# A transformer block on one core: keys scaled without a square root, one low-rank product moved, and the gate's narrow products in two row groups

## The chip, the cores and the metric

The kernel runs on one core of a Trainium2 chip. The metric is the device time of the whole launch in microseconds. A core has five engines that run side by side: TensorE (PE, with its weight loads shown as PEld), VectorE (DVE), ScalarE (ACT), GpSimd (POOL) and SyncE (SP), which mostly issues transfers. They meet only at semaphores. Products land in PSUM, which VectorE and ScalarE empty.

## The reference, cut to what matters

The block projects 512 tokens of 1024 features to many columns (float32 throughout), mixes them by a pooling branch and a recurrent branch of 16 heads of 64 features (RWKV-7), then a gate, an output product and a feed-forward part. The change lies in the recurrent branch:

```python
kk = heads(k * k_k)
kk = kk / jnp.maximum(jnp.linalg.norm(kk, axis=-1, keepdims=True), 1e-12)
k = k * (1 + (a - 1) * k_a)
o = wkv7_scan(rh, heads(decay), kh, vh, kk, heads(a))   # uses -kk and kk * a
...
w = -softplus(-(w0 + tanh(xw) @ w_decay_up)) - 0.5      # low-rank product, K = 64
a = sigmoid(a0 + xa @ w_aaa_up)                         # low-rank product, K = 64
g = sigmoid(xg) @ w_gate_up                             # low-rank product, K = 160 = 128 + 32
...
state = state * w_t + (state @ a_t) b_t + v_t k_t       # a_t = -kk, b_t = kk * a
```

## The kernel before

The recurrence is written in chunks of 64 tokens. Heads are taken four at a time, a *quad* (two pairs of 128 features, q = 0 and 1), and `QUADS` is 4. A pass `it` runs from -1 to 4 and each has 27 slots (`SLOTS`). In one pass each engine does three things: `work`, the chunk algebra of quad `it`; `prep`, the preparation of quad `it + 1` (decays, keys, scaled operands in `At`, `Bt`, `Kt`, `Rt`); and `tail`, the normalisation, the gate and the output rows of quad `it - 1`. Pass -1 has only `prep`, pass 4 only `tail`. Every engine has a function `slot(it, s)` that says what it does there, so the order on each engine is fixed by the code. Between them TensorE does the big input projection in pieces of 12 matmuls (`gemm_piece`, L1824, 128x512 in the reduced float32 form, each weight split in a high and a low part): `PER_SLOT` says how many pieces a slot has (0 to 3). ScalarE makes the high part of a weight tile (L767), GpSimd the low part (L672), and SyncE loads the raw tile.

The small products go to three PSUM buffers, `set0` to `set2`, in turn: the place of a product in `PE_ORDER` modulo 3 is its buffer, and `wait_set_free` makes TensorE wait until whoever reads the product three places earlier is done. So the list sets the order as well as who waits for whom. The names that matter here:

- `lora0`, `lora1` (L1925, L1926): the low-rank products for pair 0 and 1 of the next quad, two matmuls with 64 rows each; `lora_tanh` on ScalarE reads them (L829 into `sg`, L830 into `aa` or `aa_odd`).
- `norm0`, `norm1` (L1933): the squared norm of each head's key by a product with `ones_pair`. Then `norm_root` on ScalarE takes the square root (L837), `norm_inverse` on VectorE clips it and takes the reciprocal (L1276, L1279), and `inv0`, `inv1` on TensorE (L1943) spread the reciprocal over the 64 features. `unit_keys` (L1288) multiplies the key by it into `t1`.
- `bonus` (L1961), read by VectorE at L1399; `D`, `K`, `HD0`, `HD1`, `V1`, `K2`, `TT`, `AP0`, `AP1`: products of the chunk algebra. `K` is read by ScalarE and by VectorE (L1240, the copy with one added, called KI).
- `yT` (L1878, the turned output of the previous quad, in set 2, which `K` had before it) and `gate` (L1979 with 128 rows and L1980 with the other 32, for each q).
- `O` and `TB`, `TK` (L1866) begin a pass. `TB` and `TK` need what GpSimd makes at L704 and L705 from the prepared operands.

## Time and profile before

| | us |
|---|---|
| median of 3 runs | 1071.58 |
| the 3 runs | 1066.44, 1071.58, 1076.22 |
| the profiled execution's own time | 1063.63 |
| its span, first to last instruction | 1061.7 |
| TensorE busy in the span | 969.6 (91%) |
| VectorE, ScalarE, GpSimd busy | 687.6, 467.3, 366.6 |
| mean granted TensorE clock | 0.981 of full speed |

In the profiled execution the passes stand at: preparing pass 72 to 118 us, quad 0 118 to 209, quad 1 209 to 301, quad 2 301 to 397, quad 3 397 to 486, the tail pass to 512. What follows (gates, output product, feed-forward) takes the rest. "Busy" says only that an instruction is under way, and a matmul's end is modelled, so the waits and the start times carry more than the shares. All times below are from the span's start.

### The profile page before, as it was taken

What the parts mean: (1) busy time and instruction counts of PE and PEld (TensorE: products, weight loads), DVE (VectorE), ACT (ScalarE), POOL (GpSimd) and SP (SyncE); (2) the same over time, 40 slices, a digit from 0 to 9 for tenths busy, and PEclk for the clock granted to TensorE, in tenths of its full rate; (3) what the DMA queues carried; (4) which work ended last, traced back from release to release, by engine and by line L of the source; (5) the groups of instructions that cost most, each with busy time, mean ns of one, the idle gap of its engine ahead of it and who ended that gap; (6) DMA issues with size and microseconds to landing.
All of it is one profiled execution on the core that took longest, in us unless ns stands there. A gap on an engine that the chain in (4) does not pass through costs nothing.

```text
span 1061.7 us, 27421 instructions
## 1 busy us (share of the span) xinstructions
PE 969.6 (91%) x11539; PEld 804.7 (76%) x11539; DVE 687.6 (65%) x937; ACT 467.3 (44%) x571; POOL 366.6 (35%) x218
## 2 busy tenths in 40 slices
PE   1798989999999999899999999799999999999994
PEld 1676777777777678667688888688889898898883
DVE  5735667668847866764232255558778787787877
ACT  0335454346435623435532242374644545445351
POOL 7332510411241131124553444235144052350532
PEclk9998998999999999999999999899999999999997
DMA  9332324224332333332344328214152250432201
GB/s 370 105 99 57 89 83 144 63 81 124 92 82 82 112 86 81 114 108 61 120 135 112 128 71 253 56 48 126 35 158 76 82 158 20 138 97 61 80 1 80
DMA packets 122918, 108.03 MB, mean 102 GB/s; under 512 B 5395, under 2 KB 104641, under 8 KB 122817
## 3 DMA queue, kind: packets, MB, share of 16 engines
q1 hardware_dynamic: 113009, 83.46, 26.2%
q10 hardware_dynamic: 9808, 23.08, 7.1%
q8 instruction: 81, 1.33, 0.5%
q14 instruction: 20, 0.16, 0.0%
HBM read 100.23 MB, written 2.10 MB: 96 GB/s over the span
## 4 chain that ended last, share of the span: by engine, by line
PE 46%; issue 21%; DVE 13%; POOL 12%; ACT 3%; DMA 2%; SPq 1%; ACTq 0%; POOLq 0%; DVEq 0%
PE bank L1824 12%; POOL w_lo L737 10%; PE set L2125 6%; PE bank L2125 5%; PE set L1878 4%; PE set L2224 3%; PE set L1866 3%; PE set L1890 2%; PE bank L1805 2%; PE set L1902 1%; PE bank L2261 1%; DMA ada<-in_w_ada_dram 1%; PE bank L2224 1%; DVE Q L1240 1%; DVE acc L1176 1%
## 5 line engine op out<-in xcount | busy, mean ns | idle before, releaser
L672 POOL TENSOR_TENSOR w_lo<-w_raw,w_hi 128x1024 fp32r<-128x1024 f32 (+2 forms) x75 | 171.7, 2290 | 385.1 <-ACT w_hi L767 376.6
L767 ACT ACTIVATE w_hi<-w_raw 128x1024 fp32r<-128x1024 f32 (+2 forms) x81 | 81.8, 1010 | 104.7 <-PE set L2125 35.2
L2186 PE MATMUL set<-a_hi,w_hi 128*128 128x256 f32 x384 | 109.6, 285 | 8.1 <-DVE res L1581 5.4
L796 ACT ACTIVATE Q<-set 128x1024 f32<-128x1024 f32 x56 | 57.5, 1026 | 134.7 <-PE set L1878 69.3
L1824 PE MATMUL bank<-h_hi,w_hi 128*128 128x512 f32 x256 | 108.1, 422 | 3.5 <-POOL w_lo L672 2.6
L2186 PE MATMUL set<-a_lo,w_hi 128*128 128x256 f32 x384 | 108.6, 283 | 0.0
L2186 PE MATMUL set<-a_hi,w_lo 128*128 128x256 f32 x384 | 108.6, 283 | 0.0
L1121 ACT ACTIVATE w_hi<-w_raw 128x1024 fp32r<-128x1024 f32 x70 | 74.3, 1062 | 77.6 <-PE set L2186 63.5
L1824 PE MATMUL bank<-h_hi,w_lo 128*128 128x512 f32 x256 | 102.9, 402 | 1.0 <-issue 1.0
L1824 PE MATMUL bank<-h_lo,w_hi 128*128 128x512 f32 x256 | 103.6, 405 | 0.0
L1581 DVE SCALAR_TENSOR_TENSOR res<-set,mod,res 128x256 f32<-128x256 f32 x192 | 92.9, 484 | 14.9 <-PE set L2186 2.9
L737 POOL TENSOR_TENSOR w_lo<-w_raw,w_hi 128x1024 fp32r<-128x1024 f32 x35 | 89.5, 2557 | 9.2 <-ACT w_hi L1121 5.9
L737 POOL TENSOR_TENSOR w_lo<-w_t,w_hi 128x1024 fp32r<-128x1024 f32 x7 | 16.9, 2417 | 187.1 <-ACT w_hi L1121 187.1
L2186 PEld LDWEIGHTS set<-a_hi,w_hi 128*128 128x128 f32 x384 | 73.6, 192 | 10.1 <-issue 6.6
L2186 PEld LDWEIGHTS set<-a_lo,w_hi 128*128 128x128 f32 x384 | 73.7, 192 | 0.3
L2186 PEld LDWEIGHTS set<-a_hi,w_lo 128*128 128x128 f32 x384 | 73.6, 192 | 0.0
L1824 PEld LDWEIGHTS bank<-h_hi,w_hi 128*128 128x128 f32 x256 | 48.9, 191 | 20.1 <-issue 6.3
L1824 PEld LDWEIGHTS bank<-h_hi,w_lo 128*128 128x128 f32 x256 | 48.9, 191 | 11.3 <-issue 0.7
L1824 PEld LDWEIGHTS bank<-h_lo,w_hi 128*128 128x128 f32 x256 | 49.2, 192 | 9.6 <-issue 0.7
L1533 DVE TENSOR_TENSOR w_lo<-w_raw,w_hi 128x1024 fp32r<-128x1024 f32 x38 | 46.6, 1225 | 11.1 <-ACT w_hi L1121 7.5
L2272 PE MATMUL set<-h_hi,w_hi 128*128 128x512 f32 x128 | 49.8, 389 | 0.0
L2272 PE MATMUL set<-h_lo,w_hi 128*128 128x512 f32 x128 | 49.8, 389 | 0.0
(360 smaller groups left out, 2283.1 us busy)
## 6 DMA issues: line engine op xcount, KB each, us to landing
w_raw<-in_w_ff_dram SPq DMA_DIRECT2D x64, 512.0 KB, 4.2
w_raw<-in_w_in_dram SPq DMA_DIRECT2D x46, 512.0 KB, 3.7
y<-in_w_ada_dram ACTq DMA_DIRECT2D x20, 512.0 KB, 3.8
ada<-in_w_ada_dram SPq DMA_DIRECT2D x16, 512.0 KB, 9.2
Q<-in_w_ada_dram ACTq DMA_DIRECT2D x12, 512.0 KB, 4.1
w_raw<-in_w_rwkv_up_dram SPq DMA_DIRECT2D x8, 512.0 KB, 3.7
w_raw<-in_w_out_dram SPq DMA_DIRECT2D x8, 512.0 KB, 4.5
xtok<-in_x_dram SPq DMA_DIRECT2D x4, 512.0 KB, 9.5
```

What stands on the lines that cost most here:

```text
L672: link(pool.tensor_tensor(part_of(k, w_lo), raw_part(k), part_of(k, w_hi).bitcast(F32), ALU.subtract), "lo_ready")
L737: again(pool.tensor_tensor(w_lo[SLOT[m]][:, :, :], raw[:, :, :], w_hi[SLOT[m]][:, :, :].bitcast(F32), ALU.subtract), "lo_ready")
L767: link(act.activation(part_of(k, w_hi), raw_part(k), ACT.Copy), "hi_ready")
L796: link(act.activation(by_half(tile), psum_flat(set_of(name)), ACT.Copy), "act_kept")
L1121: link(act.activation(w_hi[SLOT[m]][:, :, :], raw[:, :, :], ACT.Copy), "hi_ready")
L1533: link(dve.tensor_tensor(w_lo[slot][:, :, :], raw[:, :, :], w_hi[slot][:, :, :].bitcast(F32), ALU.subtract), "lo_by_dve")
L1581: link(dve.scalar_tensor_tensor(out=res[:, f, tokens], in0=product, scalar=mod[:, 40 + f:41 + f], in1=res[:, f, tokens], op0=ALU.mult, op1 ...
L1824: mm = pe.matmul(o, w, hx, start=(m == 0), stop=(m == 3 * KT - 1))
L1878: mm = pe.matmul(ps[N * p:N * p + N, q, c * C:(c + 1) * C], by_pair(left, p, q, c), by_pair(right, p, q, c), start=(m == 0), stop=(m == le ...
L2125: mm = pe.matmul(o, w[slot_of(k)][:, kt, :], hx[:, kt, :], start=(kt == 0 and m == 0), stop=(kt == kts - 1 and m == 2))
L2186: mm = pe.matmul(to, wx[:, i, columns], a[:, form, i, :], start=OPENS[at] and b == 0 and i == 0 and m == 0, stop=i == 1 and m == 2, skip_g ...
L2272: mm = pe.matmul(bank[m][:, :], w[slot][:, kt, :], hx[:, kt, :], start=(kt == 0 and at == 0), stop=(kt == KT - 1 and at == 2))
```

## The change

Five edits, all in the passes:

1. ScalarE no longer takes the square root (`norm_root` is gone, eight calls). VectorE reads the squared norm from PSUM, clips it at 1e-24 and takes the reciprocal, so `inv` now carries one over the square. `t1` holds the raw scaled key over its square; `At` is the raw scaled key times the decay, and its minus sign has moved to `Bt`. The product of the two operands is the same as before.
2. VectorE's `norm_inverse` stands at the head of slot 6 (it was last in slot 6) for q = 0 and at the end of slot 12 (it was first in slot 14) for q = 1.
3. `lora1` on TensorE goes from slot 11 to slot 8, right behind `inv0` and ahead of three pieces and of `bonus`; its tanh on ScalarE goes from slot 12 to slot 8.
4. `inv1` goes from ahead of `V1` and `K2` to behind them, and `unit_keys(n, 1)` (now `keys_over_square`) behind VectorE's keeping of `K2`.
5. The gate's 32-row remainder of q = 1 lies in rows 32 to 63 (`xg1` has 64 rows, filled by one copying transfer on SyncE's queue), and both remainders are issued together after the two 128-row products.

```diff
-"D1", "KR0", "KR1", "A8T", "D2", "W0", "inv0", "bonus", "D", "lora1", "K", "HD0", "HD1", "yT", "norm1", "gate",
-"inv1", "V1", "K2", "TT", "AP0", "AP1", ...
+"D1", "KR0", "KR1", "A8T", "D2", "W0", "inv0", "lora1", "bonus", "D", "K", "HD0", "HD1", "yT", "norm1", "gate",
+"V1", "K2", "inv1", "TT", "AP0", "AP1", ...
...
-                sp.dma_start(lup[0:DG1, q, 2, :], w_gate_up[0, P:DG, cols]).then_inc(sem("gup_in"), 16)
+                sp.dma_start(lup[DG1 * q:DG1 * (q + 1), q, 2, :], w_gate_up[0, P:DG, cols]).then_inc(sem("gup_in"), 16)
...
+                if k == first_chunk(0):
+                    sp.wait_ge(sem("lora_ready"), 2)
+                    sp.dma_start(xg1[DG1:2 * DG1, :], xg1[0:DG1, :]).then_inc(sem("xg1_twice"), 16)
...
-            def norm_root(it, q):
-                m = 2 * (it + 1) + q
-                wait_made(act, f"norm{q}", it)
-                if m:
-                    act.wait_ge(sem("inverse_ready"), m)
-                link(act.activation(norms[:, :], pset[set_of(f"norm{q}")][:, 0, 0:2 * TB], ACT.Sqrt), "norm_taken")
...
-                dve.wait_ge(sem("norm_taken"), 2 * n + q + 1)
-                link(dve.tensor_scalar(norms[:, :], norms[:, :], 1e-12, None, ALU.max))
+                wait_made(dve, f"norm{q}", n - 1)
+                link(dve.tensor_scalar(norms[:, :], pset[set_of(f"norm{q}")][:, 0, 0:2 * TB], 1e-12 ** 2, None, ALU.max), "norm_taken")
...
-                    link(dve.scalar_tensor_tensor(out=a[:, h, :, 1:C], in0=kk[:, h, :, 1:C], scalar=-1.0, in1=w[:, h, :, 0:C - 1],
+                    link(dve.scalar_tensor_tensor(out=a[:, h, :, 1:C], in0=k[:, h, :, 1:C], scalar=col(90 + m), in1=w[:, h, :, 0:C - 1],
...
                 for q in range(2):
-                    o = pset[set_of("gate")][:, q, :]
-                    pe.matmul(o, lup[:, q, 1, :], xg0[:, :], start=True, stop=False)
-                    mm = pe.matmul(o, lup[0:DG1, q, 2, :], xg1[:, :], start=False, stop=True)
+                    pe.matmul(o[:, q, :], lup[:, q, 1, :], xg0[:, :], start=True, stop=False)
+                for q in range(2):
+                    rows = slice(DG1 * q, DG1 * (q + 1))
+                    mm = pe.matmul(o[:, q, :], lup[rows, q, 2, :], xg1[rows, :], start=False, stop=True)
```

On TensorE, pass 1 (quad 1) from `yT` on, before. Rows are `yT`, `norm1`, the four gate products, `inv1`, then `V1` and `K2` together, and the first matmul of the next piece:

```order
L1878 MATMUL set<-Q,O 64x64 x32
L1933 MATMUL set<-ones_pair,G 128x2 x4
L1979 MATMUL set<-xg,lup 128x512
L1980 MATMUL set<-xg,lup 128x512
L1979 MATMUL set<-xg,lup 128x512
L1980 MATMUL set<-xg,lup 128x512
L1943 MATMUL set<-ident,inverse 64x128 x8
L1866 MATMUL set<-Q 64x64 x64
L1824 MATMUL bank<-h_hi,w_hi 128x512
```

The same place now:

```order
L1869 MATMUL set<-Q,O 64x64 x32
L1924 MATMUL set<-ones_pair,G 128x2 x4
L1971 MATMUL set<-xg,lup 128x512 x2
L1974 MATMUL set<-xg,lup 128x512 x2
L1857 MATMUL set<-Q 64x64 x64
L1934 MATMUL set<-ident,inverse 64x128 x8
L1815 MATMUL bank<-h_hi,w_hi 128x512
```

The remainders have come together, and `inv1` has gone behind `V1` and `K2`.

On VectorE, pass 1 from the keeping of `K` on, before. L1240 is KI, L1269 and L1272 the decay sums, L1466 a term of the next modulation, L1276 and L1279 `norm_inverse`, L1424 and L1426 the output rows with the gate, L1288 `unit_keys`, and the last L1240 keeps `K2`:

```order
L1240 TENSOR_TENSOR Q<-set,Q 128x1024
L1269 TENSOR_SCALAR sg<-sg 128x512
L1272 SCALAR_TENSOR_TENSOR t<-scanm,sg 128x512
L1466 SCALAR_TENSOR_TENSOR y<-Q,derived,y 128x1024
L1276 TENSOR_SCALAR norms<-norms 128x8
L1279 RECIPROCAL inverse<-norms 128x8
L1424 TENSOR_TENSOR y<-y,xvb 128x1024
L1426 TENSOR_TENSOR y<-y,set 128x1024
L1466 SCALAR_TENSOR_TENSOR y<-y,derived 128x1024
L1288 SCALAR_TENSOR_TENSOR t<-G,params,set 128x512
L1240 TENSOR_TENSOR Q<-set,Q 128x1024
```

The same place now:

```order
L1231 TENSOR_TENSOR Q<-set,Q 128x1024
L1260 TENSOR_SCALAR sg<-sg 128x512
L1263 SCALAR_TENSOR_TENSOR t<-scanm,sg 128x512
L1268 TENSOR_SCALAR norms<-set 128x8
L1271 RECIPROCAL inverse<-norms 128x8
L1457 SCALAR_TENSOR_TENSOR y<-Q,derived,y 128x1024
L1415 TENSOR_TENSOR y<-y,xvb 128x1024
L1417 TENSOR_TENSOR y<-y,set 128x1024
L1457 SCALAR_TENSOR_TENSOR y<-y,derived 128x1024
L1231 TENSOR_TENSOR Q<-set,Q 128x1024
L1280 SCALAR_TENSOR_TENSOR t<-G,params,set 128x512
```

`norm_inverse` has gone ahead of the modulation term, and the keeping of `K2` ahead of the keys.

## Rows read from the trace of the kernel before

**Rows 1.** Windows: us, then busy us (count) of PE, PEld, DVE, ACT, POOL; clock, DMA, GB/s.
```profile
72.00:118.00 46.00, 41.89 (x199) 32.59 (x198) 26.84 (x38) 22.63 (x28) 16.59 (x7) 0.93 0.26 72
...
209.00:301.00 92.00, 87.92 (x2050) 67.81 (x2042) 66.67 (x81) 46.74 (x53) 22.80 (x10) 1.00 0.34 98
```
**Rows 2.** Waits of TensorE, whole span: for what, us in total, times, longest.
```profile
PE set L1943 <- issue: 4.7, 2, 3.1
PE set L1943 <- DVE inverse L1279: 4.1, 2, 2.1
PE set L1878 <- DVE Q L1240: 4.0, 3, 2.3
...
PE set L1902 <- ACT aa_odd L830: 2.5, 2, 1.3
```
**Rows 3.** Timeline, preparing pass and quad 0: start, us, engine, operation, [idle before and releaser].
```profile
87.97 0.50 PE L1824 MATMUL bank<-h_hi,w_hi 128*128 128x512 f32 x1 [2.00 <-POOL w_lo L672]
...
97.61 0.95 PE L1933 MATMUL set<-ones_pair,G 128*128 128x2 f32 x8
98.62 1.28 ACT L837 ACT_TABLE_LOAD   x1 [2.31 <-PE set L1933]
...
100.20 0.17 DVE L1276 TENSOR_SCALAR norms<-norms 128x8 f32<-128x8 f32 x1 [1.98 <-ACT norms L837]
...
100.66 0.48 PE L1943 MATMUL set<-ident,inverse 128*64 128x128 f32 x2 [2.11 <-DVE inverse L1279]
...
116.41 2.23 POOL L705 TENSOR_TENSOR Q<-Q,DC 128x1024 f32<-128x1024 f32 x1
...
118.47 0.34 PE L1866 MATMUL set<-Q 64*64 64x64 f32 x8
...
177.36 1.09 PE L1943 MATMUL set<-ident,inverse 128*64 128x128 f32 x16 [1.95 <-DVE inverse L1279]
```
**Rows 4.** Windows, columns as in Rows 1, around stretches of half clock and one without.
```profile
100.70:107.00 6.30, 6.30 (x26) 5.01 (x27) 2.99 (x6) 3.72 (x5) 2.36 (x1) 0.50 0.31 86
...
157.00:161.80 4.80, 4.77 (x16) 3.68 (x16) 1.99 (x3) 0.00 (x0) 1.58 (x1) 0.64 0.44 120
...
177.40:181.90 4.50, 4.50 (x145) 4.21 (x145) 2.16 (x2) 3.33 (x5) 1.99 (x1) 0.64 0.24 60
...
304.00:306.00 2.00, 0.20 (x13) 0.20 (x16) 0.00 (x0) 1.94 (x3) 0.00 (x0) 1.00 0.06 12
306.00:310.00 4.00, 4.00 (x95) 3.31 (x92) 1.39 (x2) 0.44 (x1) 2.40 (x1) 1.00 0.01 4
```
**Rows 5.** Timeline of quad 1, from the bonus to `yT`.
```profile
250.95 1.22 DVE L1399 TENSOR_TENSOR xvb<-set,xvb 128x1024 f32<-128x1024 f32 x1 [1.70 <-PE set L1961]
...
259.19 1.10 PE L1902 MATMUL set<-Q 64*64 64x128 f32 x32 [1.27 <-ACT aa_odd L830]
...
262.73 1.23 DVE L1240 TENSOR_TENSOR Q<-set,Q 128x1024 f32<-128x1024 f32 x1
...
264.10 1.16 PE L1878 MATMUL set<-Q,O 64*64 64x64 f32 x64 [0.86 <-DVE Q L1240]
```
**Rows 6.** Timeline of TensorE: bonus (quad 0), low-rank pair (quad 1), gate (quad 1).
```profile
161.84 1.88 PE L1961 MATMUL set<-G,ones_head 128*128 128x512 f32 x4
163.65 1.16 PE L1866 MATMUL set<-Q 64*64 64x64 f32 x64
...
217.84 0.69 PE L1925 MATMUL set<-xwa,lup 64*128 64x512 f32 x1
217.85 0.69 PE L1926 MATMUL set<-xwa,lup 64*128 64x512 f32 x1
...
266.10 1.10 PE L1979 MATMUL set<-xg,lup 128*128 128x512 f32 x2
267.14 1.12 PE L1980 MATMUL set<-xg,lup 32*128 32x512 f32 x2
...
270.30 1.09 PE L1943 MATMUL set<-ident,inverse 128*64 128x128 f32 x16
```

More of the change, by code:

```diff
@@ L84, in build @@
         w_raw += same_place(("w_raw2", [P, KT, P], F32), ("w_raw3", [P, KT, P], F32))
-        xg0, xg1 = sb("xg0", [P, S]), sb("xg1", [DG1, S])
+        xg0, xg1 = sb("xg0", [P, S]), sb("xg1", [2 * DG1, S])
         lup = sb("lup", [P, 2, 3, P])
@@ L225, in build @@
         PE_ORDER = ["TB", "TK", "O", "BR0", "BR1", "lora0", "mod", "AT0", "AT1", "TV", "AD0", "AD1", "A2T", "norm0", "A4", "A4T",
-                    "D1", "KR0", "KR1", "A8T", "D2", "W0", "inv0", "bonus", "D", "lora1", "K", "HD0", "HD1", "yT", "norm1", "gate",
-                    "inv1", "V1", "K2", "TT", "AP0", "AP1", "MR0", "MR1", "N", "OI", "S1", "S2", "S3", "S4", "S5", "S6"]
+                    "D1", "KR0", "KR1", "A8T", "D2", "W0", "inv0", "lora1", "bonus", "D", "K", "HD0", "HD1", "yT", "norm1", "gate",
+                    "V1", "K2", "inv1", "TT", "AP0", "AP1", "MR0", "MR1", "N", "OI", "S1", "S2", "S3", "S4", "S5", "S6"]
         BY_ACT = ["TB", "TK", "LT0", "LT1", "TV", "A2T", "A4T", "D1", "D2", "W0", "D", "K", "HD0", "HD1", "V1", "TT", "AP0", "N", "OI"]
@@ L896, in slot @@
                     keep_pair(b1, b2, "AP0", it)
-                if s == 14 and prep:
-                    norm_root(it, 1)
                 k = landing(it, s)
@@ L953, in slot @@
                         link(act.activation(flat_blocks(At), flat(O), ACT.Square), "o_squared")
+                    if prep:
+                        lora_tanh(it, 1)
                 if s == 10 and prep:
@@ L1303, in scaled_reads @@
                     wait_made(dve, "KR1", n - 1)
-                kk, w = (t.rearrange("p (h c t) -> p h c t", h=2, t=C) for t in (t1[:, :], t4[:, q, :]))
+                k, w = (t.rearrange("p (h c t) -> p h c t", h=2, t=C) for t in (xk[:, q, :], t4[:, q, :]))
                 a = one_g(At, q).rearrange("p h (c t) -> p h c t", t=C)
                 for h in range(2):
-                    link(dve.scalar_tensor_tensor(out=a[:, h, :, 1:C], in0=kk[:, h, :, 1:C], scalar=-1.0, in1=w[:, h, :, 0:C - 1],
+                    link(dve.scalar_tensor_tensor(out=a[:, h, :, 1:C], in0=k[:, h, :, 1:C], scalar=col(90 + m), in1=w[:, h, :, 0:C - 1],
                                                   op0=ALU.mult, op1=ALU.mult))
-                link(dve.tensor_scalar(a[:, :, :, 0:1], kk[:, :, :, 0:1], -1.0, None, ALU.mult))
+                link(dve.tensor_scalar(a[:, :, :, 0:1], k[:, :, :, 0:1], col(90 + m), None, ALU.mult))
             def scaled_writes(n, q):
@@ L1313, in scaled_writes @@
                 link(dve.scalar_tensor_tensor(out=a[:, :], in0=a[:, :], scalar=1.0, in1=t1[:, :], op0=ALU.add, op1=ALU.mult))
-                link(dve.scalar_tensor_tensor(out=one_g(Bt, q), in0=tokens(a[:, :]), scalar=0.5, in1=tokens(t3[:, :]), op0=ALU.mult, op1=ALU.mult))
+                link(dve.scalar_tensor_tensor(out=one_g(Bt, q), in0=tokens(a[:, :]), scalar=-0.5, in1=tokens(t3[:, :]), op0=ALU.mult, op1=ALU.mult))
                 link(dve.tensor_tensor(one_g(Kt, q), tokens(t2[:, :]), tokens(t3[:, :]), ALU.mult), "prepared")
@@ L1379, in slot @@
                 if s == 6:
+                    if prep:
+                        norm_inverse(n, 0)
                     if work:
@@ L1382, in slot @@
                         keep_plus_one(b4, "A4T", "A4I", it)
-                    if prep:
-                        norm_inverse(n, 0)
                 if s == 7:
@@ L1417, in slot @@
                         decay_sums(n, 1)
+                        norm_inverse(n, 1)
                 if s == 14:
-                    if prep:
-                        norm_inverse(n, 1)
                     if tail:
@@ L1427, in slot @@
                 if s == 15:
-                    if prep:
-                        unit_keys(n, 1)
                     if work:
                         keep_plus_one(b5, "K2", "K2", it)
+                    if prep:
+                        keys_over_square(n, 1)
                 if s == 16:
@@ L1973, in out_gate @@
                 pe.wait_ge(sem("lora_ready"), 2)
+                pe.wait_ge(sem("xg1_twice"), 16)
                 if it == QUADS:
@@ L1976, in out_gate @@
                 wait_set_free(pe, "gate", it)
+                o = pset[set_of("gate")]
                 for q in range(2):
-                    o = pset[set_of("gate")][:, q, :]
-                    pe.matmul(o, lup[:, q, 1, :], xg0[:, :], start=True, stop=False)
-                    mm = pe.matmul(o, lup[0:DG1, q, 2, :], xg1[:, :], start=False, stop=True)
+                    pe.matmul(o[:, q, :], lup[:, q, 1, :], xg0[:, :], start=True, stop=False)
+                for q in range(2):
+                    rows = slice(DG1 * q, DG1 * (q + 1))
+                    mm = pe.matmul(o[:, q, :], lup[rows, q, 2, :], xg1[rows, :], start=False, stop=True)
                 signal(mm, "gate", it)
@@ L2043, in slot @@
                         inverse_norm(it, 0)
+                        lora(it, 1)
                 if s == 9 and work:
@@ L2049, in slot @@
                     to_pairs("D", it, [(std(b5), b6)])
-                if s == 11 and prep:
-                    lora(it, 1)
                 if s == 12 and work:
@@ L2079, in slot @@
                         to_pairs("K2", it, [(b2, b1)])
+                    if prep:
+                        inverse_norm(it, 1)
                 if s == 17 and work:
```

11 lines of the change are left out of this document (2 added, 9 removed).

## The prediction

> **What bounds the kernel now.** I read the windows first, one for each pass. TensorE is busy 41.9 of 46 us in the preparing pass and 87.9 of 92 in quad 1, where VectorE has 66.7 and ScalarE 46.7 [rows 1]. So TensorE is the bound, and what the change can win are its own instructions, its waits, and the time in which it runs at half clock. ScalarE is half idle, so its freed time counts only where TensorE waits for it. Next come TensorE's waits by releaser: 4.1 us on `inverse` ahead of `inv1`, 4.0 on VectorE's L1240, nearly all ahead of `yT`, 2.5 on ScalarE's `aa_odd` ahead of `HD1`, and 4.7 in the middle of L1943 that nothing in the trace explains [rows 2]. Then the timeline round each of them, and the clock in windows. At full clock the pieces' matmuls run at their pace; three stretches of clock 0.50 to 0.64 (half speed, 1.2 of 2.4 GHz, for part of the window) stand behind gaps of 2.11, 3.1 and 1.95 us on TensorE, of which two are the waits for `inverse` [rows 2 to 4]. A stall of about 2 us at 304 had no such sequel: the clock stayed at 1.00 [rows 4].
>
> The parts, costed against the profiled execution (1063.63 us). It lies 8 us under the median of the three runs, 1071.58, and I know no row for those 8 us; I subtract the sum from the median.
>
> **Preparing pass.** Four things go. (a) ScalarE takes `norm0`'s root, with its table load, ahead of a weight tile in its order, and TensorE waits 2.00 us for that tile at 87.97 [rows 3]. Without the root ScalarE needn't wait for `norm0` there and saves the load's 1.28 and the root, and `lora1`, about 1.05 us, now fills the place ahead of that tile. Gain 2.0. (b) `norm1` ends at 98.56; the table load (1.28), the root and two VectorE instructions make `inv1` start at 100.66. Now VectorE reads the sums itself: from the end of the product to the end of the second instruction about 0.5 us, from L1276's 0.17 twice and the steps between. Gain 2.11 - 0.5 = 1.6. (c) The stretch of 6.30 us at half clock begins in this gap; at full clock its work takes 3.15. Gain 3.15 if the clock holds, 0 if it falls all the same. I take the gain, since the gap shrinks by three quarters. Together TensorE alone would gain 6.7. (d) But quad 0 also needs GpSimd's L705, which ends at 118.64, a sixth of a microsecond after TensorE starts `TB` and `TK` at 118.47 [rows 3]. That chain starts at `inv1`, through VectorE's keys, so it moves by what `inv1` moves: its start 3.6 earlier (2.0 + 1.6) and its length about 0.9 shorter, as it no longer runs at half clock (1.09 for the same product at 177.36, against about 2); and the second table load, ahead of ScalarE's exponents, goes too (up to 1.28). That is 4.5 to 5.5. **The gain of the pass is the smaller one: 5.0.** The ends are 2 (only one wait goes) and 6.7.
>
> A page of the Trainium skill, "ScalarE: Activation LUTs", section "What ACT_TABLE_LOAD costs", puts each switch of table set at about 2.66 us, the load of 1.28 and a drain of 1.38. Row and page agree on the load; the drain isn't here, for the load starts right behind the product it waits for and the clipping on VectorE 1.58 us after the load [rows 3]. By the page 16 loads would be 43 us of ScalarE in place of 21; the sum would be the same by either, as only the waits of TensorE enter it.
>
> **Quad 0.** The same pattern without a gate between `norm1` and `inv1`: TensorE waits 1.95 us for `inverse` at 177.36, and 4.50 us follow at a mean clock of 0.64 [rows 3, 4]. Now `V1` and `K2` (2 us) stand between the two, and `inverse` is ready about 1.7 us after `norm1`: VectorE must first end the decay sums. The wait goes. At full clock the 4.50 us hold 2.9 of work. **Gain 1.95 + 1.6 = 3.5**, between 2.0 and 3.6.
>
> **Gate, quads 0 to 3.** The four products of one gate take 4.20 us, from 266.10 to 270.30, 1.05 each, whether 128 or 32 rows [rows 6]. Afterwards there are two 128-row products in a row, as in the bonus: 1.81 us from its start to the next product's [rows 6]. Then the two remainders. The trace has no pair of 32-row products. Its nearest rows are the low-rank pair, in two groups of 64 rows, which start 0.01 apart [rows 6] and cost 1.05 in all. So a gate costs 1.81 + 1.05 = 2.86 if the remainders run side by side, a gain of 1.34; one behind the other, 1.81 + 1.81 = 3.62, a gain of 0.6. I take 1.3, as the pair is of the same kind: other rows, another PSUM bank. The page "TensorEngine Tiling (Array Packing)", section "Key Properties", says that a change of tiling mode drains TensorE, and that tiles execute in parallel. This case's rows speak for a small drain: 1.05 for a product that follows another shape against 0.9 in the bonus. By the page's word the gate wins twice, by two switches fewer and by the pairing, which is the 2.86 above.
>
> **Where the gate's gain goes.** In quad 3's pass (its `yT` belongs to quad 2) nothing of the preparation runs, and TensorE goes on with `V1` and the pieces at once: 1.3 won. In the tail pass the next thing TensorE waits for is the pool weights' transfer, issued by SyncE after GpSimd's low part of another tile; that isn't moved, so I count 0 (end: 1.3).
>
> **Quads 1 and 2: `lora1` ahead of `bonus`.** Here a wait takes another's place. `HD1` waited 1.27 us for `aa_odd` in each (set 1, which `lora1` had); now `lora1` is read long before, and that wait goes. But `bonus` comes one low-rank pair later, 1.05 us. VectorE waits for it (1.70 us at 250.95) and from there works without a break for 11.8 us until KI at 262.73, and `yT` needs KI because it takes the set of `K`: TensorE already waits 0.86 there [rows 5]. So `yT` starts 1.05 later against `bonus`'s old time, although TensorE is there 1.05 + 1.27 earlier. The wait ahead of `yT` becomes 0.86 + 1.27 + 1.05 = 3.2 us. Behind `yT` the gate is 1.3 shorter, `V1` and `K2` are free at once, and `inv1` waits for the gate's reader on VectorE (about 1.3 us after the gate's end, under `V1` and `K2`). **Net for each of the two: +1.05 - 1.3 = -0.3, together -0.5.** VectorE's earlier `norm_inverse` in slot 6 puts two instructions (0.4 us) ahead of the copy that KR0's buffer waits for; KR1 waits for ScalarE's copy anyway, so 0.1 at most, and I leave it out.
>
> **The clock behind the new wait.** A wait of 3.2 us is as long as the gap of 3.1 that was followed by half clock, 4.80 us at a mean of 0.64, a cost of 1.7; the gap of 2 us at 304 had none [rows 2, 4]. I count one fall in the two quads: +1.7. Ends: none, and two stretches as long as the one at 100.70, +3.15 each.
>
> **The rest costs nothing.** `xg1`'s copy is one transfer on SyncE's queue ahead of the loads of chunk 11, issued in the preparing pass, while the first gate stands at 266 [rows 6]; it delays one raw tile by one issue, with the tile before it already loaded. VectorE's keys have the same count and shapes, only a column in place of -1.0. ScalarE loses 8 roots and 16 table loads (26 loads become 10), under TensorE's work everywhere but in the two places above.
>
> **Sum.** -5.0 - 3.5 - 1.3 - 0 - 0.5 + 1.7 = **-8.6 us**, which is 1063.0 from the median (1055.0 from the profiled time). Some 1%, 10.7 us, is what a measurement of this kernel tells from no change.
>
> **Rivals.**
> (A) *The clock holds everywhere* (25%). Neither new wait lets it fall, the tail's 1.3 comes through, and the preparing pass gives its 6.7: -6.7 - 3.5 - 2.6 - 0.5 = -13.3, so 1058.3. For it: two of the waits that precede half clock are gone. Against it: the new wait is longer than either.
> (B) *The gaps weren't the bound* (15%). VectorE and GpSimd hold the preparing pass's end, it gives only 2, quad 0 gives its wait alone (2.0), the rest as above: -2 - 2 - 1.3 - 0.5 + 1.7 = -4.1, so 1067.5. The start of `TB` beside L705's end speaks for it.
> (C) *The remainders don't run side by side* (8%): 0.7 less in each of quads 1 to 3, 2.1 in all: -6.5, so 1065.1.
> (D) *VectorE becomes the bound from `bonus` on, and the clock pays for it: slower than before* (9%). The place is the wait ahead of `yT` in quads 1 and 2. It decides if half clock follows in both, and long, 6.3 us each (+6.3), while the preparing pass's stretch stays (its gain falls to 2), quad 0's stays too (2.0 left) and the remainders run apart (+2.1): -4 - 1.3 - 0.5 + 2.1 + 6.3 = +2.6. With the bonus late in quad 0 too (+1.05) it is about +4, so 1075. For a loss of over 1% further unexplained stalls as those in L1943 (4.7 us in two) would have to come on top; that such stalls move with any change of the instruction stream is the mechanism I can't price.
> My forecast has the other 43%.
>
> **How the numbers follow.** The cases lie between 1058 and 1075, and the scatter of the runs (1066.44 to 1076.22) is 5 us to each side; the range that leaves 2 in 10 out is 1052 to 1072. Faster by over 1%: nearly all of A and a part of the forecast, 0.39. Slower by over 1%: a small part of D, 0.07. Within 1%: the rest, 0.54.
>
> **What would show it.** Right: no gap between `norm1` and `inv1` in the preparing pass over 0.7 us, clock 1.00 from 98 to 107, and quad 0 beginning some 5 us earlier; no wait at `inv1` in quad 0; a gate of 2.9 us from its first product to the next; no wait ahead of the second `HD` and about 3 us ahead of `yT` in quads 1 and 2; ScalarE about 22 us less busy. Wrong: a gate of 3.6 us or more; half clock still there behind `norm1`; VectorE reaching KI without waiting for `bonus`; or a difference that comes from stretches after 520 us, which the change doesn't touch.

## The result, and the profile after

The changed kernel took **1078.46 us** (median of 7 runs, 1073.36 to 1079.59) against 1067.63 for the kernel before in the same round (7 runs, 1065.54 to 1076.22). The ratio is 1.008, 95% interval 1.0051 to 1.0109: slower by about 1%, where I had forecast 1063.0 and at most 1072. The profiled execution is the fastest of the seven, 1073.36 us with a span of 1071.4 and a mean clock of 0.974, against 1063.63, 1061.7 and 0.981.

First the windows of the passes, columns as in [rows 1].

```profile
72.00:118.00 46.00, 41.66 (x199) 32.50 (x198) 29.96 (x38) 17.23 (x22) 15.76 (x7) 0.93 0.26 74
118.00:209.00 91.00, 84.82 (x2108) 67.46 (x2106) 59.12 (x71) 37.42 (x43) 27.04 (x12) 1.00 0.34 99
209.00:303.00 94.00, 86.58 (x1867) 66.87 (x1866) 66.90 (x78) 39.67 (x46) 22.41 (x10) 0.96 0.33 93
303.00:407.00 104.00, 95.59 (x2060) 74.89 (x2059) 67.82 (x80) 41.14 (x47) 23.07 (x11) 0.90 0.30 85
```

ScalarE is lighter as planned (17.2 in place of 22.6 us in the first window), VectorE heavier by 3 us there. The clock column holds the news: 0.96 and 0.90 in quads 1 and 2, where it was 1.00. From `TB` to `TB`, the preparing pass ends 0.9 us later than before (119.34 against 118.47), quad 0 takes 3.5 less (86.7 against 90.25), quad 1 takes 5.6 more (98.05 against 92.5), quad 2 takes 9.0 more (104.3 against 95.3), and quad 3 with the tail 2.2 less. The 0.9 us are there before the pass begins: TensorE waits 17.1 us for its first transfer in place of 16.1, and ScalarE's high part of the same weight tile starts at 73.54 in place of 72.64. Counted from there the preparing pass takes the same in both kernels. From TensorE's last gate on the rest of the kernel takes the same (554.8 us in both).

TensorE's waits of the first 525 us (as in [rows 2]):

```profile
PE set L1869 <- DVE Q L1231: 9.3, 3, 3.6
...
PE set L1934 <- issue: 4.9, 3, 2.3
PE set L1934 <- DVE inverse L1271: 3.8, 1, 3.8
...
PE set L1857 <- DVE norms L1268: 2.0, 3, 0.8
```

The wait for `aa_odd` ahead of `HD1` is gone, the one ahead of `yT` has grown from 4.0 to 9.3 us in three, and the one for `inverse` is now a single one of 3.8. The last row is new: a product waits until VectorE has read the sums.

The preparing pass (timeline of TensorE, VectorE and GpSimd, put in order of time; [rows 3] before):

```profile
91.41 2.65 POOL L675 TENSOR_TENSOR w_lo<-w_raw,w_hi 128x1024 fp32r<-128x1024 f32 x1 [7.54 <-ACT w_hi L770]
91.84 3.01 DVE L1299 SCALAR_TENSOR_TENSOR Q<-G,params 128x252 f32<-128x252 f32 x2
94.89 2.46 DVE L1301 TENSOR_SCALAR Q<-G,params 128x8 f32<-128x8 f32 x1
94.92 2.40 POOL L675 TENSOR_TENSOR w_lo<-w_raw,w_hi 128x1024 fp32r<-128x1024 f32 x1 [0.87 <-ACT w_hi L770]
96.96 0.95 PE L1924 MATMUL set<-ones_pair,G 128*128 128x2 f32 x8
...
101.28 0.17 DVE L1268 TENSOR_SCALAR norms<-set 128x8 f32<-128x8 f32 x1
...
101.75 0.48 PE L1934 MATMUL set<-ident,inverse 128*64 128x128 f32 x2 [3.84 <-DVE inverse L1271]
...
119.34 0.87 PE L1857 MATMUL set<-Q 64*64 64x64 f32 x44
```

`norm1` ends at 97.91, yet VectorE reads the sums only at 101.28: it has no wait ahead of that row, it is behind. Its instructions ran beside GpSimd's low parts: an operation on 8 columns took 2.46 us and ended with the low part, the pair on 252 columns took 3.01 and ended 0.8 us behind the other. The same pair takes 1.00 and the same small operation 0.23 in quad 1.

Why the low parts fall there can be read on ScalarE, which makes the high part that each of them needs. The rows of the same weight tile (the tenth high part), before and now:

```profile
100.13 1.06 ACT L767 ACTIVATE w_hi<-w_raw 128x1024 fp32r<-128x1024 f32 x1
```
```profile
93.72 1.06 ACT L770 ACTIVATE w_hi<-w_raw 128x1024 fp32r<-128x1024 f32 x1 [1.70 <-PE bank L1815]
```

Before, the root of `norm1` stood ahead of this high part in ScalarE's order and held it until 100.13, when VectorE's long stretch was over. Without the root it comes 6.4 us earlier, and its low part meets VectorE (94.92). The low part of the tile before comes 1.4 us later than before (91.41 against 89.99). In the kernel before one VectorE instruction was held too: 1.98 us at 91.22 in place of 0.75.

Quad 1, from the bonus to the products behind the gate, and the gate of quad 3's pass at full clock ([rows 5, 6] before):

```profile
250.85 1.22 DVE L1391 TENSOR_TENSOR xvb<-set,xvb 128x1024 f32<-128x1024 f32 x1 [2.74 <-PE set L1952]
255.71 1.93 PE L1893 MATMUL set<-Q 64*64 64x128 f32 x64
262.81 1.22 DVE L1231 TENSOR_TENSOR Q<-set,Q 128x1024 f32<-128x1024 f32 x1
264.18 1.62 PE L1869 MATMUL set<-Q,O 64*64 64x64 f32 x64 [3.56 <-DVE Q L1231]
267.45 3.76 PE L1971 MATMUL set<-xg,lup 128*128 128x512 f32 x4
271.14 1.28 PE L1974 MATMUL set<-xg,lup 32*128 32x512 f32 x4
272.36 2.10 PE L1857 MATMUL set<-Q 64*64 64x64 f32 x128
...
464.88 1.98 PE L1971 MATMUL set<-xg,lup 128*128 128x512 f32 x4
466.79 1.13 PE L1974 MATMUL set<-xg,lup 32*128 32x512 f32 x4
467.85 2.10 PE L1857 MATMUL set<-Q 64*64 64x64 f32 x128
```

The gate takes 2.97 us at full clock (464.88 to 467.85), and 4.91 in quad 1. The stretches of half clock behind the waits, as windows ([rows 4] before):

```profile
101.70:108.00 6.30, 6.25 (x27) 5.05 (x28) 3.94 (x7) 1.58 (x3) 0.00 (x0) 0.53 0.01 3
264.10:271.20 7.10, 7.02 (x78) 4.39 (x78) 5.01 (x6) 5.15 (x6) 2.54 (x1) 0.54 0.19 68
...
367.00:381.00 14.00, 13.44 (x216) 9.19 (x218) 9.75 (x10) 6.73 (x8) 2.96 (x1) 0.51 0.30 90
```

**An account.** For each kernel I split the time from 72 us to the tail's first gate product into TensorE's idle stretches over 0.05 us (added up from its timeline), half of the time that the clock record shows at 0.50, and the rest, which is work at full clock. The wait ahead of that gate product is counted in. The windows' mean clock agrees: 0.98 over the 434.87 us of before gives 17 us at half clock, 0.96 over 444.60 gives 36.

| kernel | time in the part | idle | at half clock | work |
|---|---|---|---|---|
| before | 434.9 | 30.9 | 17.1 | 395.4 |
| changed | 444.6 | 35.6 | 34.1 | 392.0 |
| a_lora_back | 432.6 | 30.6 | 20.5 | 391.7 |
| b_lora_only | 463.0 | 36.0 | 71.7 | 391.2 |
| c_gate_only | 434.7 | 32.1 | 20.5 | 392.3 |
| d_root_only | 455.6 | 41.9 | 41.0 | 393.2 |
| i_filled | 435.7 | 28.1 | 20.5 | 397.3 |
| j_no_low | 438.5 | 32.6 | 27.3 | 392.3 |
| k_back_filled | 429.9 | 27.8 | 10.2 | 396.9 |
| l_back_norm | 429.9 | 30.6 | 10.2 | 394.2 |
| m_back_norm_ki | 449.4 | 37.8 | 41.0 | 391.1 |
| o_elsewhere | 445.8 | 31.5 | 30.7 | 398.9 |
| q_both | 431.4 | 26.3 | 17.1 | 396.6 |

Changed against before: work -3.4, idle +4.7, half clock +17.0, which costs 8.5. Together +9.7, as large as the difference of the spans. The work is shorter and the kernel slower. The last column is good to some 4 us only, for where half clock and an idle stretch overlap the time is counted in both: b_lora_only has the old gates and as much work as the kernel before, and shows 4.2 us less; i_filled has 5.6 us more than the changed kernel, and shows 5.3. Each row is one execution. That of the changed kernel is its fastest, with a clock of 0.974; its other six had 0.959 to 0.971.

### The profile page after: what moved, and what is told of

Same layout as the page of the kernel before. It is cut to its first block, busy times and chain, and to the rows that moved or that the text cites. A ratio compares the mean times of both kernels' runs of the same rounds, so it can differ in the third digit from the quotient of the medians.

```text
span 1071.4 us, 27393 instructions
## 1 busy us (share of the span) xinstructions
PE 973.1 (91%) x11539; PEld 809.7 (76%) x11539; DVE 697.9 (65%) x937; ACT 445.3 (42%) x547; POOL 367.3 (34%) x218
## 4 chain that ended last, share of the span: by engine, by line
PE 46%; issue 21%; DVE 14%; POOL 12%; ACT 3%; DMA 2%; SPq 1%; ACTq 0%; POOLq 0%; DVEq 0%
PE bank L1815 11%; POOL w_lo L740 10%; PE set L2118 6%; PE bank L2118 5%; PE set L1869 4%; PE set L2217 3%; PE set L1881 3%; PE set L1857 2%; PE bank L1796 2%; PE set L1796 1%; DMA ada<-in_w_ada_dram 1%; PE bank L2217 1%; PE set L1893 1%; PE bank L2254 1%; PE set L1934 1%
## 5 line engine op out<-in xcount | busy, mean ns | idle before, releaser
L1815 PEld LDWEIGHTS bank<-h_lo,w_hi 128*128 128x128 f32 x256 | 48.9, 191 | 10.6 <-issue 1.7
L1524 DVE TENSOR_TENSOR w_lo<-w_raw,w_hi 128x1024 fp32r<-128x1024 f32 x38 | 46.6, 1225 | 11.1 <-ACT w_hi L1112 7.5
L2265 PE MATMUL set<-h_hi,w_lo 128*128 128x512 f32 x128 | 49.8, 389 | 0.0
```

What stands on the lines that cost most here:

```text
L1524: link(dve.tensor_tensor(w_lo[slot][:, :, :], raw[:, :, :], w_hi[slot][:, :, :].bitcast(F32), ALU.subtract), "lo_by_dve")
L1815: mm = pe.matmul(o, w, hx, start=(m == 0), stop=(m == 3 * KT - 1))
L2265: mm = pe.matmul(bank[m][:, :], w[slot][:, kt, :], hx[:, kt, :], start=(kt == 0 and at == 0), stop=(kt == KT - 1 and at == 2))
```

## The experiments

Each was timed beside the kernel before, which took 1067.59 us (a, b, e, f), 1069.86 (c, d, i, j), 1069.03 (k, l, m, n) and 1069.86 (o, p, q). The first four expectations weigh three theories, W, N and S: the wait ahead of `yT` with half clock behind it; the norm operations too late on VectorE; and stalls that nothing in the trace explains.

**a_lora_back**: the changed kernel with `lora1` back.

```diff
-"inv0", "lora1", "bonus", "D", "K"
+"inv0", "bonus", "D", "lora1", "K"
-                        lora(it, 1)          # slot 8
+                if s == 11 and prep:
+                    lora(it, 1)
```

> The changed kernel with lora1 and its tanh back in their old places (slots 11 and 12, behind D); all else as changed. Theory W (the wait ahead of yT): lora1 ahead of bonus makes VectorE's chain from the bonus to KI late, TensorE waits 3.6 us for it in quads 1 and 2, and half clock follows. Then the wait shrinks to about 2.2 us or less, split between HD1 and yT, half clock in quads 1 and 2 is mostly gone, and the time falls about 8 to 14 us below the changed kernel, that is 1064 to 1070, at or below before. Theory N (the norm operations): the loss comes from VectorE reading the norms late (3.8 us ahead of inv1 in the preparing pass, 0.8 ahead of K2); then the time stays within 3 us of the changed kernel, 1075 to 1079. Theory S (the unexplained stalls that move with the instruction stream): any value between, with the stalls' sum (about 11 us before, 14 after) explaining it.

1063.68 us (12 runs), ratio to before 0.9947 (0.9922 to 0.9972): 14.8 us faster than the changed kernel. The waits ahead of `yT` are 1.05 us, those for `aa_odd` ahead of `HD1` 1.26 again. The move of `lora1` is what made the change slow; the other four edits gain 4 us.

**b_lora_only**: the kernel before with that move alone.

> The kernel before with lora1 and its tanh moved alone. Theory W: the wait ahead of yT grows from 0.9 to about 3.2 us in quads 1 and 2 with half clock behind it, no gain from the gate: 8 to 14 us slower than before, 1076 to 1082. Theory N: same as before within 3 us, 1066 to 1071. Theory S: no telling, with the sum of the unexplained stalls showing it.

1090.48 us (6 runs), ratio 1.0181 (1.0138 to 1.0223). Its waits and windows behind the two `yT`s:

```profile
PE set L1878 <- DVE Q L1240: 9.3, 3, 3.4
PE set L1943 <- DVE inverse L1279: 7.1, 2, 5.0
```
```profile
269.60:286.70 17.10, 16.93 (x224) 10.50 (x224) 7.81 (x10) 6.36 (x8) 2.75 (x1) 0.50 0.34 101
378.80:392.50 13.70, 13.70 (x116) 7.35 (x120) 6.53 (x8) 5.49 (x8) 2.75 (x1) 0.50 0.26 77
```

That is 8 us above the range of theory W. The two waits are those of the changed kernel (3.38), the half clock behind them lasts far longer, and there are more waits with half clock behind them that W had not foreseen: 5.0 us ahead of `inv1` in quad 0 (6.8 us of it) and 2.56 ahead of quad 3's `yT` (13.7). The idle sum grows by 5.1 us only; the clock costs 27.

**e_ki_early**: the changed kernel, KI ahead of `scaled_writes`.

```diff
-                if s == 11 and prep:
-                    scaled_writes(n, 0)
-                if s == 12:
+                if s == 11:
                     if work:
                         keep_plus_one(b4, "K", "KI", it)
+                    if prep:
+                        scaled_writes(n, 0)
```

> The changed kernel with VectorE's KI (and ScalarE's keeping of K, ahead of one transfer's issue) moved ahead of the three scaled writes and one modulation term, so that KI comes about 3 us earlier while lora1 stays ahead of bonus. Theory W: the wait ahead of yT falls from 3.6 to under 1 us, the half clock behind it goes, and the time falls 8 to 14 us, to 1064 to 1070. Theory N: unchanged within 3 us. Theory S: change only as the stalls' sum changes.

1077.96 us (11 runs), ratio 1.008 (1.0053 to 1.0107): nothing. The wait ahead of `yT` went and came back behind the gate:

```profile
PE set L1935 <- DVE y L1418: 7.8, 2, 3.9
```

L1418 is the gate's reader. From the bonus to it VectorE works through one chain, so what `yT` no longer waits for, `inv1` does. Theory W in its first form, that the place of the wait matters, fell.

**f_pieces**: the changed kernel, three of the weight products' pieces moved from slot 15 to slot 12, so that they run in the wait ahead of `yT`.

```diff
-PER_SLOT = [2, 1, 0, 3, 3, 0, 1, 2, 3, 0, 3, 0, 3, 0, 0, 3,
+PER_SLOT = [2, 1, 0, 3, 3, 0, 1, 2, 3, 0, 3, 0, 6, 0, 0, 0,
```

> The changed kernel with the three pieces of slot 15 moved to slot 12, ahead of yT: TensorE works 2.8 us where it waited. Theory W: the wait ahead of yT falls to about 0.8 us, TensorE's clock holds there, and 5 to 12 us are won, if nothing behind slot 15 waits for VectorE in turn (TT needs K2, which VectorE keeps late; that could give back 2 us a quad). Theory N: unchanged or slower. Theory S: as the stalls fall.

1069.86 us (12 runs), ratio 1.0016 (0.9992 to 1.004): 8.6 faster than the changed kernel. The waits ahead of `yT` are 0.85 and 0.84; new ones of 1.5 to 1.9 us, and one of 3.6 in quad 3's pass, stand behind the gate, where the pieces are missing.

**i_filled**: useless work in the same wait. Nothing that waits is released earlier.

```diff
-both_to_heads("HD1", it, b6, b3, IB)
+both_to_heads("HD1", it, b6, b3, IB, 4 if it in (1, 2) else 1)
```

> The changed kernel, with HD1's 64 products issued four times over in quads 1 and 2 (the same values into the same places), so that TensorE works through about 2.8 of the 3.56 us in which it waited ahead of yT. Nothing that waits is released earlier. Theory W (most of what lora1's move costs is half clock behind that wait): the wait ahead of yT shrinks to 0.8, half clock behind it (6.8 us in quad 1, 20.5 in quad 2 in the profile of the changed kernel) goes for the most part, and the kernel gets 5 to 12 us faster for doing more: 1066 to 1073 against 1078. Theory V (the waits themselves, and VectorE's chain, are the cost): the time stays within 2 us of the changed kernel's, 1076 to 1080, or is longer.

1063.29 us (12 runs), ratio 0.9936 (0.9901 to 0.9971). With 5.6 us more of work (six rounds of 0.93) the changed kernel gets **15.2 us faster**. No wait is left ahead of `yT` (stalls of 1.4 and 1.2 us in the repeated rounds, which nothing in the trace explains, took the rest of it), and the places that ran at half clock run at full:

```profile
264.10:271.20 7.10, 7.10 (x99) 4.94 (x90) 5.49 (x7) 3.72 (x5) 0.00 (x0) 1.00 0.34 106
364.00:378.00 14.00, 14.00 (x309) 10.33 (x308) 12.47 (x15) 7.91 (x9) 4.89 (x2) 1.00 0.49 158
```

The medians differ by 15.2 us. The two profiled executions differ by 7.4 only (1073.36 and 1065.98), the one the fastest of its kernel, the other slower than its median; so the account, which shows 8.9 us between them, doesn't explain the whole of the 15.2.

**p_one_round**: one extra round of `HD1` instead of three.

> The changed kernel with one extra round of HD1's products in quads 1 and 2 in place of three: 0.93 us, so the wait ahead of yT shrinks from 3.56 to about 2.6 us. Theory L (the length of the wait decides how long half clock lasts behind it): a part of the 15 us of three rounds comes back, 4 to 11 us, 1067 to 1074, with half clock behind yT shorter than the 6.8 and 20.5 of the changed kernel. Theory M (only a wait that is nearly gone leaves the clock up): 1076 to 1079. Theory C (any change of the stream shifts the stalls): 1067 or less.

1069.81 us (12 runs), ratio 0.9999 (0.9975 to 1.0023): 8.7 faster than the changed kernel. The waits are 2.69 and 2.36 us, followed by 6.8 and 3.4 us of half clock:

```profile
264.60:271.70 7.10, 7.07 (x78) 4.44 (x78) 4.96 (x6) 5.15 (x6) 2.54 (x1) 0.55 0.21 71
362.20:369.30 7.10, 7.10 (x112) 3.80 (x115) 4.68 (x7) 5.15 (x6) 3.09 (x1) 0.76 0.19 68
```

The time is as theory L had it. Half clock shortened in quad 2 alone (13.7 to 3.4); in quad 1 it is as long as in the changed kernel. So the list of all the waits ahead of `yT` in quads 1 and 2 says more, with the half clock that starts within 2.5 us of their end: under 0.1 us (e, i, k, m and q): none in ten; 0.84 to 1.05 us (before, f_pieces, and a, c, d, l and n): one stretch of 3.4 in fourteen; 2.36: 3.4; 2.69: 6.8; 3.38 to 3.56 (changed, b, j, o): 6.8 to 17.1 in all eight. Between these lie the waits ahead of `yT` in quad 3's pass, 2.20 to 2.56 us in fourteen kernels: no half clock in six (before and changed among them), 3.4 in seven, 13.7 in one. So a longer wait has half clock behind it more often and for longer, but the same wait has it in one kernel and not in another.

**k_back_filled**, the control: `lora1` back, and the three extra rounds.

> The control for the filled wait: the changed kernel with lora1 back in its old place (1063.7 us on its own), and the same three extra rounds of HD1's products in quads 1 and 2. There the wait ahead of yT is 1.04 us, so of the 2.8 us of extra work 1.8 lie on the path in each quad. Theory W (the extra rounds gained by filling a long wait, and only so): 3 to 5 us slower than without them, 1066.5 to 1069. Theory X (extra work on TensorE there helps whatever it fills, or the 15 us were a shift of stalls that no edit controls): as fast as without them or faster, 1064 or less.

1059.57 us (12 runs), ratio 0.9907 (0.9881 to 0.9933): 4.1 **faster** than a_lora_back, where W wanted 3 to 5 slower. By the account work grew by 5.2, but idle time fell by 2.8 and half clock by 10.3 us. The fills took 1.05 us of wait twice; of the clock, most was won in places that no edit touched (a stretch at 214 and two in quad 3's pass). So W's "and only so" fell: some 4 us come where there is hardly a wait to fill.

The four kernels together part the two effects. Without the rounds the move of `lora1` costs 14.8 us (1063.68 to 1078.46), with them 3.7 (1059.57 to 1063.29). The difference, 11.1 us, hangs on the long wait; by the four intervals it is good to some 6 us.

**o_elsewhere**, the second control: the changed kernel, `lora0`'s pair six times over where TensorE doesn't wait.

```diff
+                for again in range(5 if q == 0 and it in (1, 2) else 0):
+                    pe.matmul(ps[:, 0, :], lup[0:DW, q, 0, :], xwa[0:DW, :], start=True, stop=True)
+                    pe.matmul(ps[:, 1, :], lup[DW:P, q, 0, :], xwa[DW:P, :], start=True, stop=True)
```

> The changed kernel with extra work on TensorE where it does not wait: lora0's pair six times over in quads 1 and 2 (the same values into the same places), some 2.7 us each, at about 215 and 313 in the profile of the changed kernel. Theory W (extra rounds gain only where they fill a wait): 3 to 6 us slower than the changed kernel, 1081 to 1085. Theory X (extra rounds gain wherever they stand): faster than it by 3 us or more, under 1075.

1076.65 us (10 runs), ratio 1.0069 (1.004 to 1.0098). Neither: no 15 us as from the fill, but no loss either, though there is more work than I had meant. The five extra rounds take 4.4 us in each quad (TensorE, 214.82 to 219.22 in quad 1), 8.8 in all and not 5.4. The waits of 3.56 stayed, and half clock behind them:

```profile
266.70:273.80 7.10, 7.10 (x78) 4.45 (x80) 5.18 (x6) 5.16 (x6) 2.78 (x1) 0.55 0.20 70
371.90:383.50 11.60, 11.60 (x203) 7.49 (x207) 8.96 (x8) 6.18 (x7) 2.80 (x1) 0.56 0.32 101
```

So extra work as such doesn't bring the 15 us of i_filled: 11 of them, as parted above, belong to the filled wait. Beside that there is a give and take between kernels, in unexplained stalls and in stretches of half clock elsewhere. It is large: k_back_filled is some 8 us and this kernel some 10 us faster than their extra work on the path would have them (an estimate: 5.6 - 2.1 + 4.1 = 7.6, and 8.8 + 1.8 = 10.6).

**j_no_low**: the changed kernel, two of GpSimd's low parts in the preparing pass cut to an eighth; the rest of those two tiles' low parts is not computed.

> The changed kernel, with two of GpSimd's low parts of weight tiles in the preparing pass (the ones at 91.41 and 94.92, 2.65 and 2.40 us) cut to an eighth of their columns: seven eighths of those two tiles' low parts are not computed. Theory G (VectorE's instructions beside a GpSimd operation are stretched to its end, and that holds up norm_inverse in the preparing pass): L1299's pair takes 1.0 in place of 3.01 and L1301 0.23 in place of 2.46; norm_inverse comes up to 4.2 us earlier and the wait of 3.84 ahead of inv1 falls under 1 us; half clock at 101 goes with it or shortens; quad 0 begins 3 to 7 us earlier, and the kernel is at 1071 to 1075 against 1078. Theory Q (VectorE's order alone is late, decay sums and scaled writes ahead of norm_inverse): the two instructions are stretched all the same or the wait stays over 2.5 us, quad 0 begins less than 1.5 us earlier, and the time stays at 1077 to 1079.

1069.74 us (12 runs), ratio 0.9995 (0.9966 to 1.0025): 8.7 faster than the changed kernel. The same instructions of VectorE (a line further down), then `inv1` and `TB`, then the window behind it:

```profile
91.43 1.08 DVE L1300 SCALAR_TENSOR_TENSOR Q<-G,params 128x252 f32<-128x252 f32 x2
92.55 0.23 DVE L1302 TENSOR_SCALAR Q<-G,params 128x8 f32<-128x8 f32 x1
...
97.32 1.09 PE L1935 MATMUL set<-ident,inverse 128*64 128x128 f32 x16 [0.60 <-DVE inverse L1272]
...
112.37 2.41 PE L1858 MATMUL set<-Q 64*64 64x64 f32 x128
```
```profile
97.30:103.60 6.30, 6.28 (x39) 5.22 (x40) 4.78 (x9) 3.31 (x5) 0.22 (x1) 1.00 0.25 75
```

Theory G holds; the time is 1.3 us under its range. The wait is 0.60, the clock holds, and quad 0 begins 7.0 us earlier than in the changed kernel, 6.1 earlier than before: what I had forecast for this pass (5.0, end 6.7) was there, behind the stretched instructions.

**l_back_norm**: `lora1` back; in the preparing pass `norm_inverse` ahead of the decay sums.

```diff
-                    if prep:
+                    if prep and work:
                         decay_sums(n, 1)
                         norm_inverse(n, 1)
+                    elif prep:
+                        norm_inverse(n, 1)
+                        decay_sums(n, 1)
```

> The changed kernel with lora1 back in its old place, and in the preparing pass alone the second norm_inverse ahead of the decay sums on VectorE. Without it VectorE is at the decay sums when norm1 ends (96.4), and they are stretched beside GpSimd to 2.59 us. Theory G: norm_inverse then follows norm1 by less than 1.9 us in place of 3.1, inv1's wait falls from 3.37 to under 2.1, quad 0 begins 1 to 2 us earlier, and half clock there shortens or stays: 1060 to 1063. Theory T (the decay sums, now later, hold up ScalarE's exponents and the keys of set 1, so quad 0's start does not move): 1063.5 to 1065.

1061.46 us (12 runs), ratio 0.9927 (0.99 to 0.9954), 2.2 under a_lora_back, which the two intervals alone don't tell from nothing; the trace does. VectorE now waits for the sums, and `inv1` starts 0.57 us behind them; quad 0 begins at 115.36 in place of 117.30, and no half clock follows.

```profile
97.44 0.17 DVE L1268 TENSOR_SCALAR norms<-set 128x8 f32<-128x8 f32 x1 [1.12 <-PE set L1927]
...
97.90 1.09 PE L1937 MATMUL set<-ident,inverse 128*64 128x128 f32 x16 [0.57 <-DVE inverse L1271]
```

**m_back_norm_ki**: the last one with the edit of e_ki_early.

> As the last one, and KI ahead of scaled_writes on VectorE (and K's copy ahead of the loads on ScalarE). Theory W: the wait of 1.04 ahead of yT goes in quads 1 and 2, and inv1 behind the gate waits 1 us or less for y_ready, since the low-rank pair stands before HD1 and TensorE is later at yT; 0 to 2 us faster than the last one. Theory Y (VectorE from the bonus to y_ready is one chain, and what yT gains inv1 loses): the same time as the last one within 1.5 us, with a wait for DVE y ahead of inv1 of 1 us or more in quads 1 and 2.

1072.15 us (12 runs), ratio 1.0039 (1.0008 to 1.007): 10.7 **slower** than without KI's move, far outside both theories. The waits of 1.05 ahead of `yT` went, and this came:

```profile
PE set L1938 <- DVE y L1421: 6.0, 2, 3.0
```

Half clock grew from 10.2 to 41.0 us in eleven short stretches. Behind the two new waits stand 3.4 us each, so with the 3.9 us by which they are longer than those they replaced they account for 7.3 us. The other nine stretches lie elsewhere, and I can't explain them. (The profiled execution, 1078.15, is one of the slower ones.)

**n_back_inv**: `lora1` back, and `inv1` ahead of `V1` and `K2` again (VectorE's keys ahead of K2's copy with it).

> The changed kernel with lora1 back in its old place and inv1 ahead of V1 and K2 again (edit 4 undone, VectorE's keys of set 1 ahead of K2's copy with it). It prices the move of inv1. As I predicted for quad 0: inv1 there waits 1.3 to 2 us for VectorE, half clock behind it, 2 to 3.5 us slower than without this edit: 1065.5 to 1067.5. Theory Z (the move of inv1 is worth nothing, the wait in quad 0 was hidden elsewhere): within 1 us, 1063 to 1064.7.

1062.83 us (12 runs), ratio 0.9939 (0.9914 to 0.9965), 0.9 under a_lora_back, within the noise. The move of `inv1` is worth nothing: without it `inv1` waits 0.80 us in quad 0, where before it waited 1.95 [rows 3].

**d_root_only**: the kernel before with the keys without a root, every operation at its old place.

> The kernel before with the keys without a root (edits 1 and part of 2), every place of an operation as before: VectorE reads the sums from PSUM where norm_inverse stood, lora1 stands where it stood. Theory R (my prediction's sums for the parts that need no move): the wait of 2.0 for the weight tile in the preparing pass goes, the waits ahead of inv1 shrink from 2.1 and 1.95, some 3 to 6 us won: 1062 to 1065. Theory N (VectorE is the releaser in the preparing pass, so taking ScalarE away only moves the wait): inv1 still waits 2 to 3.5 us there, and quad 0 begins no more than 1 us earlier; won are 1 to 3 us: 1065 to 1067. ScalarE's busy time falls by about 22 us in either.

1086.19 us (6 runs), ratio 1.0155 (1.0097 to 1.0213), the second slowest of all, 16 us slower than before where both theories had a gain. Its waits:

```profile
PE set L1855 <- DVE norms L1265: 10.5, 3, 4.0
PE set L1932 <- DVE inverse L1268: 7.4, 2, 4.0
```

ScalarE used to read the sums as soon as they were there. Now VectorE reads them where `norm_inverse` stands, and until then the PSUM set isn't free for the product three places behind `norm0`: 2.8, 3.7 and 4.0 us in quads 0 to 2, where the changed kernel has 0.8 at most. And `norm_inverse` late in quad 0 keeps `inv1` waiting 4.0 us, where n_back_inv, with the same keys and `inv1` at the same place, has 0.80. That VectorE's operations went to earlier places (edit 2) was no detail.

**c_gate_only**: the kernel before with the gate's edit alone.

> The kernel before with the gate's edit alone (edit 5 of the diff). Two theories of the gate's worth. P (the remainders run side by side and the bound is TensorE): each gate takes 2.9 us in place of 4.2 at full clock; 1.3 us won in the passes of quads 1, 2 and 3, some 3 to 4 us in all, so about 1064 against 1067.6. H (the shorter gate is eaten by what waits behind it): the gate is 1.3 shorter but inv1 then waits for VectorE (y_ready, the gate's reader), as it did in the run with KI ahead; nothing is won outside quad 3, at most 1.3 in all, 1066 to 1068.

1065.89 us (12 runs), ratio 0.9966 (0.9933 to 0.9998), and work is 3.1 us less in the account (three gates by 1.3 would be 3.9):

```profile
263.09 1.96 PE L1983 MATMUL set<-xg,lup 128*128 128x512 f32 x4
264.98 1.13 PE L1986 MATMUL set<-xg,lup 32*128 32x512 f32 x4
266.04 1.09 PE L1946 MATMUL set<-ident,inverse 128*64 128x128 f32 x16
```

2.95 us a gate, and `inv1` behind it did not wait: theory P.

**q_both**: l_back_norm with the three extra rounds.

> The two edits that gained on top of the changed kernel with lora1 back in its old place, in one kernel: the second norm_inverse ahead of the decay sums in the preparing pass (1061.5 alone), and the three extra rounds of HD1's products in quads 1 and 2 (1059.6 alone), against 1063.7 with neither. They act in different passes. Theory A (their gains add): 1056 to 1058.5. Theory C (each gain was a shift of stalls and of half clock, not the edit's own): 1060 to 1064.

1057.85 us (6 runs), ratio 0.9897 (0.986 to 0.9935): the fastest, 1% faster than the kernel before, and the gains of k and l add. Its 5.6 us of repeated products are included.

## Why the prediction was wrong

- **"The clock behind the new wait"** is the step that failed. I forecast the wait ahead of `yT` well (3.2 against 3.56 us in both quads), and counted one fall, +1.7, with ends of 0 and +6.3. In the profiled execution 6.8 and 13.7 us of half clock follow, half of which is +10.2, and quads 1 and 2 take 14.6 us longer where the prediction had 1.2 (-0.5 and +1.7). The measured price of the whole move is +14.8 us (against a_lora_back), and filling the wait gives back 15.2, of which 11 belong to the wait. I had sized the fall by a gap of 3.1 us with 1.7 behind it, and held a gap of 2 us without a sequel against more; [rows 4] also had the 6.30 us at 0.50 behind a gap of 2.11, and I used that only as an end. Rival D named the mechanism and put 9% on it, at 1075.
- **"Preparing pass", part (b)** failed too: -5.0 became 0 (the 0.9 us by which it ends later are there at its start). I let VectorE read the sums right behind `norm1`, but the order has the decay sums and the scaled writes ahead of it, which I noted for quad 0 and not here. In the trace of before VectorE had ended them at 98.2 and stood idle; in the changed kernel GpSimd's low parts fall on VectorE's busy stretch, one of them because the root no longer holds ScalarE's high part back, and VectorE reads the sums 3.4 us after they are there. Removing the collision gave 7.0 us. With (b) the clock of (c) failed: 6.8 us of half clock follow the wait, as before. Part (a) and the table loads were right: the wait at the weight tile is gone, and ScalarE is 22.0 us less busy (445.3).
- **Quad 0**: -3.5 forecast, -3.5 measured, for the wrong reason in part. `V1` and `K2` between the two weren't needed; the missing root and the earlier `norm_inverse` together did it (0.80 us of wait in n_back_inv, 4.0 in d_root_only without the latter). That the sum agrees is luck: both stretches of half clock are gone (3.4 us each, a gain of 1.7 each), of which I had forecast one, and an unexplained stall of 0.9 us stands where the wait was.
- **Gate**: 2.86 forecast, 2.97 and 2.95 measured; the remainders run side by side. Rival C is out.
- **"VectorE's earlier `norm_inverse`"** I costed at nothing. The root's removal without it cost 16 us (d_root_only), with it nothing of the kind: it frees the PSUM set and makes `inverse` early. No run has this edit alone.
- **Tail**: 0 as forecast; 1.6 us of wait for the pool weights stands in the gate's place.
- **Open**: why the stretches of half clock and the unexplained stalls away from the waits shift by up to some 10 us from kernel to kernel (k_back_filled, o_elsewhere, m_back_norm_ki), and why the same wait of 2.2 us has half clock behind it in one kernel and not in another.

## What to carry to other kernels

Where TensorE is the bound, price a wait by the half clock behind it, not by its own length: here waits of 1 us had it behind them once in fourteen, waits of 2.2 to 2.6 us in nine of fifteen, and the move that made two waits of 3.56 us cost 15. Before a releaser is taken away from one engine, list what that engine freed early (here a PSUM set) and read on the new engine's row order when it will get there. And ask what the relieved engine will do earlier, and whom that meets: here a weight tile came 6.4 us sooner and its low part held up VectorE. And test a suspected clock cost by filling the wait with repeated work; it needs no other edit, and the result can be used.
